# A fused decoder step: the last pair of up tiles by seven products, and one weight rounding placed later at the start

## The reference, cut to what matters

```python
h2 = _rmsnorm(x, g_ffn)
f = jnp.einsum("btd,df->btf", h2, w_up)              # 1024 -> 2 x 2816
f_gate, f_up = jnp.split(f, [D_FF], axis=-1)
f_conv, new_f = _causal_dwconv(f_gate, buf_f, conv_f_w)   # 3 taps
x = x + jnp.einsum("btf,fd->btd", jax.nn.silu(f_conv) * f_up, w_down)
```

## Time and profile before

| | us |
|---|---|
| median of 3 runs | 836.84 |
| lowest, highest | 836.80, 837.04 |
| the profiled execution | 836.67 |
| its span | 834.9 |
| TensorE busy | 825.1 |
| VectorE busy | 713.9 |
| ScalarE busy | 449.7 |
| GpSimd busy | 165.5 |

### The profile page before, as it was taken

The page is one execution under the profiler, slowest core; times in us unless marked ns, Lnnn a source line. Parts: engine busy times, 40 slices in busy tenths (PEclk is TensorE's granted clock), DMA queues, the critical chain, the costliest instruction groups (busy, mean ns, idle before and its releaser), DMA issues.

```text
span 834.9 us, 18079 instructions
## 1 busy us (share of the span) xinstructions
PE 825.1 (99%) x6836; PEld 822.1 (98%) x6836; DVE 713.9 (86%) x1072; ACT 449.7 (54%) x814; POOL 165.5 (20%) x138
## 2 busy tenths in 40 slices
PE   8999999999999999999999999999999999999996
PEld 7999999999999999999999999999999999999996
DVE  6899898989999976766569899999999998967775
ACT  7753636454333234665236576667766666533553
POOL 2283737566000000000002210000000002500000
PEclk9999999999999999999999999999999999999999
DMA  9424223442342342235933116555554554335663
GB/s 264 128 79 117 84 83 93 134 118 88 101 116 83 100 113 76 84 94 70 202 107 102 50 45 171 127 127 127 132 134 115 140 126 136 99 87 116 138 139 106
DMA packets 191614, 95.02 MB, mean 114 GB/s; under 512 B 34552, under 2 KB 187020, under 8 KB 191524
## 3 DMA queue, kind: packets, MB, share of 16 engines
q1 hardware_dynamic: 183921, 86.02, 38.7%
q0 software_dynamic: 3456, 6.29, 4.4%
q10 hardware_dynamic: 4171, 1.82, 0.8%
HBM read 83.79 MB, written 3.51 MB: 105 GB/s over the span
## 4 chain that ended last, share of the span: by engine, by line
PE 94%; DVE 3%; issue 1%; DMA 1%; ACT 0%; SPq 0%; DVEq 0%; ACTq 0%
PE psum L2133 36%; PE psum L2139 18%; PE psum L2303 17%; PE psum L2308 9%; PE psum L2436 6%; PE psum L2442 3%; PE psum L2331 2%; PE psum L2336 1%; DMA raw<-in_w_in 1%; PE psum L2508 1%; PE psum L2176 1%; PE psum L2183 0%; PE psum L2174 0%; DVE w_lo L1623 0%; PE psum L2525 0%
## 5 line engine op out<-in xcount | busy, mean ns | idle before, releaser
L2133 PE MATMUL psum<-act,w_hi 128*128 128x260 f32 x1984 | 258.6, 283 | 0.0
L2133 PEld LDWEIGHTS psum<-act,w_hi 128*128 128x128 f32 x1984 | 246.3, 188 | 0.0
L2139 PE MATMUL psum<-act,w_lo 128*128 128x260 f32 x992 | 139.9, 283 | 0.0
L1317 DVE TENSOR_TENSOR w_lo<-raw,w_hi 128x1024 fp32r<-128x1024 f32 x78 | 103.1, 1323 | 34.8 <-ACT w_hi L718 34.5
L2139 PEld LDWEIGHTS psum<-act,w_lo 128*128 128x128 f32 x992 | 128.0, 188 | 0.0
L647 POOL TENSOR_TENSOR gate_a<-gate_a,prods 128x512 f32<-128x512 f32 x72 | 108.8, 1512 | 81.4 <-ACT prods L797 73.3
L2303 PE MATMUL psum<-act,w_hi 128*128 128x260 f32 x768 | 121.4, 282 | 0.0
L2303 PEld LDWEIGHTS psum<-act,w_hi 128*128 128x128 f32 x768 | 105.6, 188 | 0.0
L1623 DVE TENSOR_TENSOR w_lo<-raw,w_hi 128x1024 fp32r<-128x1024 f32 (+1 forms) x68 | 81.8, 1203 | 15.6 <-ACT w_hi L985 15.6
L718 ACT ACTIVATE w_hi<-raw 128x1024 fp32r<-128x1024 f32 x78 | 81.9, 1053 | 21.0 <-PE psum L2139 16.7
L985 ACT ACTIVATE w_hi<-raw 128x1024 fp32r<-128x1024 f32 (+1 forms) x68 | 69.6, 1030 | 37.0 <-PE psum L2308 23.9
(11 more groups left out here) (272 smaller groups left out, 1312.7 us busy)
## 6 DMA issues: line engine op xcount, KB each, us to landing
raw<-in_w_in SPq DMA_DIRECT2D x56, 512.0 KB, 3.7
raw<-in_w_up SPq DMA_DIRECT2D x44, 512.0 KB, 4.2
raw<-in_w_down SPq DMA_DIRECT2D x16, 448.0 KB, 3.9
w_lo<-raw POOLq DMA_DIRECT2D x24, 256.0 KB, 3.3
v<-in_x_prompt SPq DMA_DIRECT2D x8, 512.0 KB, 7.5
raw<-in_w_b_out SPq DMA_DIRECT2D x8, 512.0 KB, 4.0
raw<-in_w_a_out SPq DMA_DIRECT2D x8, 512.0 KB, 5.9
raw<-in_w_o SPq DMA_DIRECT2D x8, 512.0 KB, 4.3
```

The source lines that it names most:

```text
L1317: ve.tensor_tensor(w_lo[:, slot, 0:k, :], raw[:, s, 0:k, :], w_hi[:, slot, 0:k, :], ALU.subtract).then_inc(lo_done, 1)
L2133: pe.matmul(a[:, h, :], w_hi[:, s, j, :], rhs(k, part)[:, h * H:(h + 1) * H], start=start and part == 0, stop=False)
L2139: last = pe.matmul(a[:, h, :], w_lo[:, s, j, :], rhs(k, 0)[:, h * H:(h + 1) * H], start=False, stop=stop)
```

## The change

`PLAIN` becomes `(0,)`: pair 21 goes by seven products. Its bank for P1, P6, P7 and P4 is bank 0. P4 of pair 21 is issued within `down_plain(0)`, behind three of its tiles. Step 20 is now an ordinary step within the run on all engines, with four weight sums for pair 21, and the code behind the loop takes in the pieces of pair 21. `down_plain(0)` gets a wait for the product of pair 20, `down_plain(1)` one for the product of pair 21, and GpSimd waits for P3 of pair 21 where it waited for the end of pair 21.

At the head, VectorE makes the first two low parts of h between the two weight halves.

```diff
-    PLAIN = (0, 21)
+    PLAIN = (0,)
...
                 if j == KH - 1:
-                    pool.wait_ge(p_done, PRODUCT["up", FT - 1])
+                    pool.wait_ge(p_done, PRODUCT["P3", FT - 1])
...
                 if j == 0:
-                    pool.wait_ge(p_done, PRODUCT["up", FT - 1])
+                    pool.wait_ge(p_done, PRODUCT["P3", FT - 1])
...
+            def up_hi_after(name, first, last):
+
+                sc.wait_ge(p_done, PRODUCT[name, FT - 1])
+                for i in range(first, last):
+                    up_hi(i)
+
...
+            hi_4(FT - 1)
+            up_1(FT - 1)
             conv_first(FT - 2)
-            for i in range(EARLY_HI, EARLY_HI + 2):
-                up_hi(i)
-            hi_up(FT - 1)
+            hi_3(FT - 1)
+            hi_open(FT)
             silu(FT - 2)
-            for i in range(EARLY_HI + 2, EARLY_HI + 6):
-                up_hi(i)
-            hi_open(FT)
+            up_v(FT - 1)
+            up_hi_after("P6", EARLY_HI, EARLY_HI + 2)
+            up_5(FT - 1)
+            up_hi_after("P6", EARLY_HI + 2, EARLY_HI + KH)
+            up_hi_after("P5", EARLY_HI + KH, EARLY_HI + 2 * KH - 1)
             conv_first(FT - 1)
-            for i in range(EARLY_HI + 6, EARLY_HI + 8):
-                up_hi(i)
+            up_hi_after("P5", EARLY_HI + 2 * KH - 1, EARLY_HI + 2 * KH)
+            up_hi_after("P7", EARLY_HI + 2 * KH, KD)
+            hi_up(FT)
             silu(FT - 1)
-            for i in range(EARLY_HI + 8, KD):
-                up_hi(i)
-            hi_up(FT)
...
             second_half(0)
+            for at in range(2):
+                h_lo_split(0, at)
             second_half(1)
-            for at in range(KT):
+            for at in range(2, KT):
                 h_lo_split(0, at)
...
+            def up_los(first, last):
+
+                for i in range(first, last):
+                    up_lo(i)
+
             up_gate(FT - 2)
+            lo_2(FT - 1)
             conv_rest(FT - 2)
+            lo_3(FT - 1)
+            lo_open(FT)
             up_product(FT - 2)
-            lo_up(FT - 1)
-            for i in range(EARLY_HI, EARLY_HI + 4):
-                up_lo(i)
-            plain_gate(FT - 1)
-            lo_open(FT)
+            up_los(EARLY_HI, EARLY_HI + 2)
+            up_22(FT - 1)
+            up_los(EARLY_HI + 2, EARLY_HI + 4)
+            up_gate(FT - 1)
+            up_los(EARLY_HI + 4, EARLY_HI + 6)
             conv_rest(FT - 1)
-            for i in range(EARLY_HI + 4, EARLY_HI + 6):
-                up_lo(i)
-            plain_product(FT - 1)
-            for i in range(EARLY_HI + 6, KD):
-                up_lo(i)
+            up_los(EARLY_HI + 6, EARLY_HI + 7)
+            up_product(FT - 1)
+            up_los(EARLY_HI + 7, KD)
             lo_up(FT)
...
+            pe.wait_ge(prod_done, START + 2 * KT + FT - 1)
             down_plain(0)
             turn_tail_f()
-            pe.wait_ge(cx_set, FT)
+            pe.wait_ge(prod_done, START + 2 * KT + FT)
             down_plain(1)
```

More of the change, by code:

```diff
@@ L391, in build @@
         assert not any(FOLLOWS[FT:]) and not SEVEN[-1]
-        assert PLAIN[0] == 0 and PLAIN[-1] == FT - 1 and SEVEN[1]
-        BANK_X = {1: 2, 2: 3, 3: 0, 4: 1, 5: 2, 6: 3, 7: 0, 8: 1, 9: 2, 10: 3, 11: 0, 12: 1, 13: 2, 14: 3, 15: 0, 16: 1, 17: 2, 18: 3, 19: 2, 20: 3}
-        BANK_GATE = {0: 0, 21: 0}
+        assert PLAIN == (0,)
+        BANK_X = {1: 2, 2: 3, 3: 0, 4: 1, 5: 2, 6: 3, 7: 0, 8: 1, 9: 2, 10: 3, 11: 0, 12: 1, 13: 2, 14: 3, 15: 0, 16: 1, 17: 2, 18: 3, 19: 2, 20: 3, 21: 0}
+        BANK_GATE = {0: 0}
         assert len(BANK_X) + len(BANK_GATE) == FT
@@ L441, in hi_step @@
         def hi_step(n):
-            if n >= FT - 1:
+            if n >= FT:
                 return down_step(n)
@@ L1180, in _ @@
                     step_at_end_of_run(n)
+            hi_4(FT - 1)
+            up_1(FT - 1)
             conv_first(FT - 2)
-            for i in range(EARLY_HI, EARLY_HI + 2):
-                up_hi(i)
-            hi_up(FT - 1)
+            hi_3(FT - 1)
+            hi_open(FT)
             silu(FT - 2)
-            for i in range(EARLY_HI + 2, EARLY_HI + 6):
-                up_hi(i)
-            hi_open(FT)
+            up_v(FT - 1)
[3 more added lines that the diff above has]
+            up_hi_after("P5", EARLY_HI + KH, EARLY_HI + 2 * KH - 1)
             conv_first(FT - 1)
-            for i in range(EARLY_HI + 6, EARLY_HI + 8):
-                up_hi(i)
+            up_hi_after("P5", EARLY_HI + 2 * KH - 1, EARLY_HI + 2 * KH)
+            up_hi_after("P7", EARLY_HI + 2 * KH, KD)
+            hi_up(FT)
             silu(FT - 1)
-            for i in range(EARLY_HI + 8, KD):
-                up_hi(i)
-            hi_up(FT)
-            sc.wait_ge(p_done, PRODUCT["up", FT - 1])
+            sc.wait_ge(p_done, PRODUCT["P3", FT - 1])
             sc.dma_start(gf_row[:, :], g_final.rearrange("(o d) -> o d", o=1).broadcast_to([P, D])).then_inc(gf_in, 16)
```

## The result

| | median us | lowest to highest | ratio to before, 95% interval |
|---|---|---|---|
| before, 6 runs | 836.94 | 836.33 to 837.72 | |
| after, 6 runs | 842.12 | 841.73 to 843.37 | 1.0062 [1.0051, 1.0072] |

The forecast was 840.2 with a range of 837.3 to 841.6. The sign is right, the size is not: 5.2 us instead of 3.4. The time lies in the band of rival (3), 841.3 to 842.5, but neither of that rival's two causes is what the profiles show. The profiled execution of after is its slowest, 843.37 us with a span of 841.6, against 836.67 and 834.9 for the profile of before. So the two profiles differ by 6.7 us, and 1.5 us of that has to be something that a typical run has not.

The account below looks back on a forecast made before the run. TensorE, busy 99% of the span, was taken to bound the kernel, with VectorE's lateness the risk. Saved matmuls -1.44, waiting +4.5 and head +0.35 gave +3.4 us, so 840.2, range 837.3 to 841.6.

Parts of the forecast that it names:

- rival (3): More than one place: ScalarE's last rounding adds its own delay, or the sums slow further; 841.3 to 842.5, chance 0.07.
- TensorE's part, -1.44: Pair 21: 96 matmuls removed and 84 added, 12 x 0.120 = 1.44 us less for TensorE.
- VectorE up to `up_22`: End of up stage: GpSimd's first three sums delay VectorE's taps and `lo_3`, so `up_22` comes at 702.7, not 701.8.
- Each operation of VectorE waits out a sum, 0.55 us more: Behind `up_22`: nine VectorE operations with two SBUF inputs each wait for a GpSimd sum, 9 x 0.55 = 5.0 us.
- the low product forecast to be 4.5 us late: In `down_plain(0)`: the second weight tile's low part, needed at 712.4, comes at 716.9; TensorE waits 4.5 us in pieces.
- (1): Rival: VectorE's operations mostly slip past GpSimd's sums, nothing waits, not slower: 835.7, or 834.9 with a head gain; chance 0.17.
- (2): Rival: only half the turns are taken, a wait of 1.5 to 3.5 us: 837.3 to 839.2; chance 0.14.
- `down_plain(1)` and the new wait ahead of `down_plain(0)`, nothing: Down stage: the products of pairs 21 and 20 are ready before TensorE needs them, so these waits cost nothing.
- The head, +0.35: Head: GpSimd's low parts start later and TensorE waits ahead of `first_lo(1, 0)`; a loss of 0.35 us, not a 0.54 gain.
- the sum itself: Whole kernel: TensorE's saving -1.44, its waiting for VectorE +4.5 and the head +0.35 make +3.4 us, 840.2.

Follow-up runs that it names:

- kernel without waits: Against the kernel before: pair 21 by seven products, old head, GpSimd's sums from the fourth on held back, VectorE's late token low parts moved behind weight low parts; 835.86 us.
- the pair alone: Pair 21 by seven products with the head left as in the kernel before; 841.46 us against 837.08, ratio 1.0056.
- filled kernel: Pair 21 by seven products, old head, plus 6, 7 and 17 unused transposes ahead of TensorE's three waits; 839.78 us, ratio 1.0033 to the kernel before.

## Why the prediction was right and where it failed

**TensorE's part, -1.44: right.** 12 matmuls less on the page, and 1.3 us in the kernel without waits.

**VectorE up to `up_22`: right in the total.** Forecast 702.7; 703.95 in the profile, less the head's 1.17, is 702.8. The delay was not one turn at each of three operations, though: the two taps alone took 3.0 us instead of 1.55, and `lo_3` lost nothing. No wait at P4 nor at the start of `down_plain(0)`, and ScalarE's last rounding was done at 710.3, ahead of TensorE's second half at 710.65. So neither place of rival (3) came, though the measured time lies in its band.

**"Each operation of VectorE waits out a sum, 0.55 us more": right in kind, a little too large.** Nine turns were counted, 5.0 us; the operations lost 4.3. The low part of tile 8 slipped through ahead of the sum, and the second product half lost only 0.20. So the low product forecast to be 4.5 us late was 4.0 late, in the three pieces named. With the sums out of the way the delays are gone, which shows the cause. Rivals (1) and (2) fall.

**`down_plain(1)` and the new wait ahead of `down_plain(0)`, nothing: right.**

**The head, +0.35: not to be told from zero.** The mechanism is in the rows of one profile (GpSimd 0.4 us later, and eight products that wait for it), where what VectorE's earlier low parts give and what that takes come to +0.16. The term is over-sized. In the profile of after itself the wait did not come, since TensorE was slower there than GpSimd.

**The step that failed is the sum itself:** "-1.44 + 4.5 + 0.35 = +3.4" prices a wait of TensorE at its length. There was no term for what TensorE does behind the wait. With the clock at half behind three waits, that is 1.5 to 1.7 us in the pair alone (timeline, and filled kernel), and 2.7 us in the profile of after. In its place the sum reads -1.44 + 4.1 + 1.5 to 2.7 + 0 = 4.2 to 5.4, and 5.2 was measured. Two errors in the other direction (0.4 at the waits, 0.2 to 0.35 at the head) hid part of it; that the miss is no larger is luck. The range was too narrow for the same reason: its upper end, 841.6, rested on the lengths of waits alone.

**What stays open.** Why the half clock lasted 6.8 us in the one profile and 3.4 in the two others is not settled. How often it lasts so long isn't known either, since only one run of each kernel was profiled, nor whether it accounts for the 0.7 us between after and the pair alone. The three waits have the same lengths in both. It was also not tried where between 1.55 and 4.45 us a single wait begins to cost the clock.

## What to carry to other kernels

When an edit makes TensorE wait several microseconds in one place, price the wait and the slow matmuls behind it, and read the granted clock of the stretch behind it first. Before filling the last free microseconds of VectorE, look at what GpSimd runs beside it: here token sums that nobody needed soon cost the critical low parts 4.3 us, and holding them back until the last of these was made brought the time back to that of the kernel before. When a wait has been removed, look where it went: here it moved twice, from tile to tile, before the saved matmuls could be seen in the time.

## What the runs showed of the hardware that was not expected

- TensorE's granted clock went from 2.4 to 1.2 GHz at the end of waits of 0.77, 0.9 and 2.1 us in a row, and at the end of one of 4.45 us, for 3.4 to 6.8 us; it stayed at 2.4 behind one of 1.55 us, and behind the same three places when transposes filled them.
- In the first 15 us the old head ran at full pace in one profile (before: matmuls 0.12 apart from 11.6 on) and with a granted clock of 0.51 from 8.1 to 15 in another (no wait left), with the end about 1.1 us later than in that kernel's other runs. In the profile of after the matmuls there stood 0.21 apart while the granted clock read 1.00.
- The first matmul behind a wait lasted 0.39 us instead of 0.28, also where transposes filled the wait (12 matmuls 1.70 us instead of 1.60); three waits cost 0.3 us in this way.
- A rounding of VectorE with one SBUF input and no PSUM (128x512) waited for GpSimd as well: 1.46 us instead of 0.42.
